# Reordered work at the seams of the 15-product passes and the down groups of a hybrid trunk kernel

## The reference, cut to what matters

```python
def swiglu(x, w_gate, w_up, w_down):
    return (jax.nn.silu(x @ w_gate) * (x @ w_up)) @ w_down
...
    h = x + 0.5 * swiglu(rmsnorm(x, ffn1_norm), ffn1_w_gate, ffn1_w_up, ffn1_w_down)
    p = rmsnorm(h, mix_norm) @ w_in
```

## Time and profile before

| what | us |
|---|---|
| runs | 1909.55, 1913.75, 1920.72 (median 1913.75) |
| profiled execution, device time | 1914.03 |
| its span | 1911.2 |
| first stage, until PE stops | 183.6 |
| passes, from PE's first matmul to the last | 197.28 to 518.8 |
| down groups | 518.8 to 840.3 |
| all behind them | 840.3 to 1911.2 |

### The profile page before, as it was taken

The page is one execution under the profiler, slowest core; times in us unless marked ns, Lnnn a source line. Parts: engine busy times, 40 slices in busy tenths (PEclk is TensorE's granted clock), DMA queues, the critical chain, the costliest instruction groups (busy, mean ns, idle before and its releaser), DMA issues.

```text
span 1911.2 us, 31212 instructions
## 1 busy us (share of the span) xinstructions
PE 1778.4 (93%) x11761; PEld 1755.1 (92%) x11761; DVE 1293.3 (68%) x2145; ACT 680.0 (36%) x1269; POOL 772.6 (40%) x767
## 2 busy tenths in 40 slices
PE   8998799999767777799999999999999999999998
PEld 8998799999657777799999999999999999999998
DVE  7264677776755555466257755997778877887775
ACT  7211444444322222235221153543333333333333
POOL 2697455555383233321079812223323333233320
PEclk9999899999878888899999999999999999999999
DMA  5432223222522022124811170111111111112112
GB/s 151 167 117 87 83 72 91 77 64 92 188 78 78 25 84 80 56 67 175 153 35 46 55 226 12 51 45 52 53 52 51 50 51 51 55 45 61 45 41 104
DMA packets 182358, 151.43 MB, mean 79 GB/s; under 512 B 11538, under 2 KB 175698, under 8 KB 181188
## 3 DMA queue, kind: packets, MB, share of 16 engines
q1 hardware_dynamic: 176724, 141.80, 24.3%
q0 software_dynamic: 864, 5.28, 0.8%
q10 hardware_dynamic: 4624, 2.36, 0.5%
HBM read 117.86 MB, written 31.57 MB: 78 GB/s over the span
## 4 chain that ended last, share of the span: by engine, by line
PE 74%; POOL 11%; DVE 5%; DMA 4%; issue 3%; ACT 2%; SPq 0%; DVEq 0%; POOLq 0%; ACTq 0%
PE bank_pair L1502 20%; PE bank_pair L1504 20%; PE bank_pair L1503 20%; PE bank_down L1502 4%; PE bank_down L1504 4%; PE bank_down L1503 4%; POOL PROD L3757 3%; DMA GW_raw<-in_ffn_w_down 3%; POOL UF_raw L3896 1%; POOL BS L3757 1%; POOL CA L3757 1%; ACT GS_hi L2329 1%; DVE GH_lo L3098 1%; POOL GS_raw L3903 1%; POOL TMP L3757 1%
## 5 line engine op out<-in xcount | busy, mean ns | idle before, releaser
L1502 PE MATMUL bank_pair<-XHM,U_hi 128*128 128x344 f32 x720 | 230.4, 320 | 0.2 <-DVE XLM L2870 0.2
L1504 PE MATMUL bank_pair<-XHM,U_lo 128*128 128x344 f32 x720 | 229.7, 319 | 0.0
L1503 PE MATMUL bank_pair<-XLM,U_hi 128*128 128x344 f32 x720 | 229.7, 319 | 0.0
L1502 PEld LDWEIGHTS bank_pair<-XHM,U_hi 128*128 128x128 f32 x720 | 135.2, 188 | 0.6 <-DVE XLM L2870 0.5
L1503 PEld LDWEIGHTS bank_pair<-XLM,U_hi 128*128 128x128 f32 x720 | 135.2, 188 | 0.0
L1504 PEld LDWEIGHTS bank_pair<-XHM,U_lo 128*128 128x128 f32 x720 | 135.2, 188 | 0.0
L1502 PE MATMUL bank_pair<-XF_hi,UF_hi 128*128 128x344 f32 x340 | 111.4, 328 | 21.7 <-DVE UF_lo L3033 13.7
L1502 PE MATMUL bank_pair<-GH_hi,GS_hi 128*128 128x344 f32 x160 | 59.5, 372 | 69.0 <-DVE HT L3120 69.0
L1502 PE MATMUL bank_pair<-XH,WH 128*128 128x344 f32 x384 | 123.6, 322 | 0.1
L3240 DVE SCALAR_TENSOR_TENSOR HT<-bank_pair,HT 128x344 f32<-128x344 f32 x210 | 103.5, 509 | 28.3 <-PE bank_pair L1504 28.0
L1503 PE MATMUL bank_pair<-XL,WH 128*128 128x344 f32 x384 | 122.5, 319 | 0.0
(11 more groups left out here) (487 smaller groups left out, 5855.3 us busy)
## 6 DMA issues: line engine op xcount, KB each, us to landing
GW_raw<-in_ffn_w_down SPq DMA_DIRECT2D x20, 512.0 KB, 3.5
GH_raw<-h_scratch SPq DMA_DIRECT2D x25, 344.0 KB, 6.0
RAW<-in_w_in SPq DMA_DIRECT2D x16, 512.0 KB, 4.3
UN<-in_ffn_w_gate SPq DMA_DIRECT2D x30, 256.0 KB, 3.6
UN<-in_ffn_w_up SPq DMA_DIRECT2D x30, 256.0 KB, 3.1
DQ_raw<-in_ffn_w_down SPq DMA_DIRECT2D x30, 256.0 KB, 2.8
h_scratch<-SA SPq DMA_DIRECT2D x40, 172.0 KB, 2.0
U_raw<-in_ffn_w_gate SPq DMA_DIRECT2D x22, 256.0 KB, 2.9
```

What stands on the lines that cost most here:

```text
L1502: pe.matmul(out, wh, xh, start=first, stop=False, skip_group_check=onto)
L1503: pe.matmul(out, wh, xl, start=False, stop=False, skip_group_check=onto)
L1504: return pe.matmul(out, wl, xh, start=False, stop=last, skip_group_check=onto)
```

## The change

It reorders the lists of all engines around three places and moves one piece of work.

- The turns of table C go from POOL to DVE (`c_turn`, eight of them, between the muls of f = 1 and 2). DVE's reciprocal moves ahead of the muls of f = 1. SP stores table C, and loads the first raw units inside its loop over f. POOL makes the table of powers behind table B instead of behind the fourth quarter.
- The last DVE and ACT items of the first stage make the parts of the first three steps; the five late x forms are spread over the first eight steps. In each step copies and adds come before the parts, and muls lag one step. R12 is before R11.
- In the last steps the group's first parts come one step later or more, SP's loads and stores of the last pass are in a list of their own, and in the groups ACT and DVE take the sums of quarter k+1 instead of k+2, ACT with quarter_high(k+2) behind group_high. BY_POOL is empty; the instructions that go by it are not made.

```diff
-PASS_ORDER = ("R1", "R2", "R9", "R4", "R6", "R3", "R7", "R0", "R5", "R8", "R13", "R14", "R11", "R12")
+PASS_ORDER = ("R1", "R2", "R9", "R4", "R6", "R3", "R7", "R0", "R5", "R8", "R13", "R14", "R12", "R11")
...
-FINALS = {"R6": ((1, 0),), "R3": ((0, 0),), "R5": ((1, 1),), "R8": ((0, 2),), "R11": ((2, 1),), "R12": ((1, 2), (2, 2)),
+FINALS = {"R6": ((1, 0),), "R3": ((0, 0),), "R5": ((1, 1),), "R8": ((0, 2),), "R11": ((2, 1), (2, 2)), "R12": ((1, 2),),
...
+BY_POOL = ()
+GROUP_LOW = tuple(u for u in GROUP_FORMS if u not in BY_POOL)
...
+C_TURNS = 4 + 6 * 8
...
+            for f in range(FO):
+                if f + 1 < FO:
+                    load_first(0, f + 1)
+                    load_first(1, f + 1)
...
+                if f == 3:
+                    sp.wait_ge(c_done, C_TURNS)
+                    sp.dma_start(CAD, CA[:, :, :, :].rearrange("p g r n -> p (g r) n")).then_inc(ca_out, 16)
+                if f == FO - 2:
+                    sp.wait_ge(ca_out, 16)
+                    sp.wait_ge(bs_out, 32)
+                    for at in range(5):
+                        load_raw(0, at)
...
+            run_past("R1")
+            load_ht(0, 0, 2)
+            run_past("R9")
+            load_group_h(0, B22)
...
+            run_past("R3")
+            load_group_h(0, B11)
+            load_group_h(0, B21)
+            store_h(LAST, 0, 0)
+            run_past("R7")
+            load_group_w(0)
+            run_past("R0")
+            load_group_h(0, None)
+            store_h(LAST, 0, 1)
+            store_h(LAST, 1, 1)
...
+            run_past("R12")
+            load_ht(2, 5, DC)
+            run_past("R11")
+            load_group_h(0, B13)
+            sp.wait_ge(un_ready, len(RUN))
+            load_group_h(0, B23)
+            store_h(LAST, 2, 1)
+            store_h(LAST, 2, 2)
+            run_past(TAIL)
+            load_group_w(1)
+            for u in (B11, None, B22, B21):
+                load_group_h(1, u)
+            store_h(LAST, 2, 0)
             for m, j in ((0, 0), (2, 1), (2, 0)):
                 wait_stored(sp, m, j, TRIPLES)
             load_group_w(2)
...
                 if name == "R0":
-                    act.wait_ge(ca_out, 16)
+                    act.wait_ge(bs_out, 32)
                 if name == "R9":
                     act.wait_ge(w_split[1], FO)
...
                     silu(f, (0,))
                     if f == 1:
                         discretise()
+                    if f == 6:
+                        for i in range(3):
+                            run_hi(i)
                     silu(f, (1, 2))
-                    if f == 6:
-                        x_form_hi("R0")
...
-            for i in range(3):
-                run_hi(i)
-            x_form_hi("R13")
-            x_form_hi("R10")
             run_hi(3)
             tail = len(RUN)
+            late = {0: "R13", 1: "R10", 3: "R8", 5: "R11", 6: "R12"}
             for i in range(tail):
...
                 if i + 4 < tail:
                     run_hi(i + 4)
-                run_copies(i)
...
-                    x_form_hi("R12")
...
+                if i in late:
+                    x_form_hi(late[i])
+                if i == tail - 5:
                     quarter_high(0)
-                if i == tail - 5:
+                if i == tail - 4:
                     group_high(0, B11)
+                if i == tail - 3:
+                    group_high(0, T1)
                     sums_high(0)
...
+                if i == tail - 2:
                     group_high(0, B21)
-                if i == tail - 3:
                     group_high(0, T2)
-                    group_high(0, B22)
...
+            quarter_high(1)
             for k in range(4 * GROUPS):
                 g, q = divmod(k, 4)
-                if k == 0:
-                    quarter_high(1)
-                    sums_high(1)
-                if k + 2 < 4 * GROUPS:
-                    quarter_high(k + 2)
-                    sums_high(k + 2)
+                if k + 1 < 4 * GROUPS:
+                    sums_high(k + 1)
                 if g + 1 < GROUPS and q > 0:
                     for u in GROUP_FORMS[3 * (q - 1):3 * q]:
                         group_high(g + 1, u)
+                if k + 2 < 4 * GROUPS:
+                    quarter_high(k + 2)
                 if k == 4 * GROUPS - 2:
...
+            def c_turn(n):
+
+                cr, ci = (AP8[:, 7, what, :].rearrange("p (g o) -> p g o", o=1).broadcast_to([P, GP, C16]) for what in range(2))
+                x, y = (CA[:, :, ri, (n - 1) * C16:n * C16] for ri in range(2))
+                before = 4 + 6 * (n - 1)
+                dve.wait_ge(c_done, before)
+                for out, part, turn in zip(CTMP, (x, y, y, x), (cr, ci, cr, ci)):
+                    dve.tensor_tensor(out[:, :, :], part, turn, ALU.mult).then_inc(c_done, 1)
+                dve.wait_ge(c_done, before + 2)
+                dve.tensor_tensor(CA[:, :, 0, n * C16:(n + 1) * C16], CTMP[0][:, :, :], CTMP[1][:, :, :], ALU.add
+                                  ).then_inc(c_done, 1)
+                dve.wait_ge(c_done, before + 4)
+                dve.tensor_tensor(CA[:, :, 1, n * C16:(n + 1) * C16], CTMP[2][:, :, :], CTMP[3][:, :, :], ALU.subtract
+                                  ).then_inc(c_done, 1)
+
...
                 dve.wait_ge(disc_p, 2)
                 dve.reciprocal(TMP[:, 12, :], TMP[:, 7, :]).then_inc(den_inv, 1)
+                c_turn(1)
+                c_turn(2)
+                mul(1, 0)
+                c_turn(3)
+                mul(1, 1)
+                c_turn(4)
+                mul(1, 2)
                 first_split(1, 2)
+                for n in range(5, 9):
+                    c_turn(n)
                 first_split(0, 3)
-                for tb in range(TB):
-                    mul(2, tb)
-                first_split(1, 3)
...
                 x_restore("B00", 0, 0)
+                mul(2, 0)
                 x_restore("B10", 1, 0)
                 x_step("R3", raw["R3"], b["B10"], b["B00"], "B10")
+                mul(2, 1)
                 x_restore("B02", 0, 2)
                 x_step("R7", raw["R7"], b["B02"], b["B00"], "B02")
-                first_split(0, 4)
...
                 first_split(1, 4)
                 x_form_lo("R3")
                 x_form_lo("R7")
                 x_restore("B01", 0, 1)
+                dve.wait_ge(bs_out, 32)
...
                 first_split(0, 5)
-                dve.wait_ge(bs_out, 32)
...
                 x_form_lo("R9")
                 x_form_lo("R0")
-                mul(6, 1)
-                run_lo(0)
-                run_lo(1)
-                mul(6, 2)
+                for i in range(2):
+                    run_lo(i)
+                for tb in range(TB):
+                    mul(6, tb)
+                run_lo(2)
...
             ffn_first()
-            x_form_lo("R13")
...
             tail = len(RUN)
...
+                run_adds(i)
                 if i + 3 < tail:
                     run_lo(i + 3)
-                run_adds(i)
-                if i == 0:
-                    x_form_lo("R8")
-                if i == 1:
...
+                if i in late:
+                    x_form_lo(late[i])
+                if i > 0:
...
+                    run_muls(i - 1)
                 if i == tail - 5:
                     group_mix(0, T1)
+                if i == tail - 4:
                     group_low(0, B11)
-                if i == tail - 4:
                     group_mix(0, T2)
+                if i == tail - 3:
                     group_mix(0, T4)
+                    group_low(0, T1)
+                if i == tail - 2:
+                    group_mix(0, T3)
                     sums_low(0)
-                if i == tail - 3:
-                    group_mix(0, T3)
-                    group_low(0, T1)
-                    group_low(0, B21)
-                if i == tail - 2:
-                    group_low(0, T2)
-                    group_low(0, B22)
-            group_low(0, B13)
-            group_low(0, B23)
-            group_low(0, T3)
-            group_low(0, T4)
+            run_muls(tail - 1)
+            for u in GROUP_LOW[2:]:
+                group_low(0, u)
             for n in range(GROUP_STEPS):
                 k, name = GROUP_RUN[n]
                 g, q = divmod(k, 4)
                 group_add(n)
-                if name == "M1" and k == 0:
-                    sums_low(1)
-                if name == "M3" and k + 2 < 4 * GROUPS:
-                    sums_low(k + 2)
+                if name == ("M3" if k else "P2") and k + 1 < 4 * GROUPS:
+                    sums_low(k + 1)
                 if g + 1 < GROUPS:
...
-            for j in range(1, 9):
-                rotate(ca(0, j), ca(1, j), ca(0, j - 1), ca(1, j - 1), ar, ai, -1)
-
-            pool.dma_start(CAD, CA[:, :, :, :].rearrange("p g r n -> p (g r) n")).then_inc(ca_out, 16)
+            pool.wait_ge(c_done, C_TURNS)
+
...
+            square_of((t(3), t(4)), t(5), t(6))
...
```

(41 more changed lines are left out.)

173 lines of the change are left out of this document (63 added, 110 removed).

## The result

The changed kernel takes **1822.3 us** (median of 4 runs, 1821.4 to 1824.7); the kernel before took 1913.0 in the same comparison (4 runs, 1909.6 to 1920.7). The ratio is 0.9523, with a 95% interval of 0.9492 to 0.9553: 91 us off, where 121 were forecast.

What follows compares the result with a forecast made beforehand. PE, busy 93% of the span, was taken as the bound, its losses mostly in groups and passes. Terms -96.5 + 15 - 13.7 - 10.7 - 6.9 - 9.9 = -122.7 from 1914.0 gave 1792 us, range 1768 to 1828.

Steps and rivals of the forecast that it cites:

- rival 2: Down groups: VectorE, not PE, sets the quarter at 12 us; 32 us more, 1824 us; chance 0.15.
- Groups, -96.5: Down groups: reordered ACT and DVE lists let PE set quarters of 10.3 us; 225 us with extras, against 321.5.
- C table, +15: First stage: turns moved to DVE cost 5.0 us each beside POOL, making the stage 15 us late; bounds 0 to +27.
- Rival 1: First stage: turns are cheap, 2.3 us each, and the stage is not late; 1777 us; chance 0.25.
- the two forecast stops: First stage: PE waits for FW_lo behind the turns, 3.2 us in tile 2, then until the stage is 13.6 us late.
- Behind it DVE has slack: First stage after the turns: DVE works 25.5 of 45.3 us, so the lateness is passed on and doesn't grow.
- Gap ahead of the passes, -13.7: Between first stage and passes: PE goes straight from the last up tile into R1, so the 13.7 us gap goes.
- Passes, -10.7, -6.9 and -9.9: Ten passes: PE's losses fall to 7 us at the start, 2 from 300 to 500, and 2.5 at the end.
- SP's queue is rewritten here: End of the passes: SP's reordered loads and stores hold back group 1's loads, wanted only 18 us later; no cost.
- Nine low parts by VectorE, nothing: Down groups: all nine low parts being DVE's is no edit, since BY_POOL is empty; no gain or loss.
- Rivals 2 and 3: Rival 3: both the longest turns in the first stage and somewhat late quarters in the groups; 1819 us; chance 0.07.
- Rival 4: Down groups: the loop through the weight load doesn't open, quarters of 16.5 us and more; 1925 us; chance 0.015.

Runs made afterwards that it cites:

- run 4: Changed kernel with the down groups' lists on ACT and DVE back to two quarters ahead, all else kept: 1908.7 us, against 1822.3 for the changed kernel.
- Run 5: Changed kernel with SyncE issuing the loads of B13 and B23 ahead of HT's load: 1815.7 us, against 1822.3 for the changed kernel.
- run 3: Changed kernel with POOL starting its B table only when all eight turns of the C table are done: 1823.1 us, against 1822.3.
- run 7: Changed kernel with turns 7 and 8 moved behind later low parts and FW_lo of tile 4 moved forward: 1806.0 us, against 1822.3.
- run 1: Changed kernel with SyncE issuing the sixth raw load of the next pass ahead of the store of block (1,2): 1808.0 us, against 1822.3.
- Runs 10 and 11: Changed kernel with load ahead, HT last, turns spread, later T2 form; low parts T3 and T4 on GpSimd (10) or all nine on VectorE (11): 1790.3 and 1790.5 us.

## Why the prediction was partly right

The direction and the mechanism that carries it were right, the size was 30 us too good. The measured time lies within the stated range, 1768 to 1828, only because of the bound that rival 2 set; the forecast by itself reached from 1780 to 1806. Point by point, by the sum:

- **Groups, -96.5.** It was -87.2, and undoing the order of ACT's and DVE's lists alone gives back 86 us (run 4). PE sets the quarter inside a group: from 550 to 600 us it makes 306 matmuls at clock 1.00 with one stop of 1.67 us, so a quarter of 66 takes 10.4 us, forecast 10.3. Of the miss of 9.3 us, 7.8 are at the start, a term that was named and mis-sized. The prediction had B13 and B23 behind HT, but took 8.5 us and 1.6 for the clock in all. Measured, from 513.17 to 550 us, PE lost 36.8 - 121 x 0.1565 = 17.9: the stops at 515.22, 517.57, 527.42 and 539.99 are 0.94 + 1.17 + 8.67 + 2.12 = 12.9, the other 5.0 are matmuls at the lower clock (0.77 granted in this stretch). Run 5 shows the share of the queue in it. Three of the four group changes cost 1.67, 1.98 and 1.50 us, close to the 1.5 forecast for each, the fourth nothing; there SyncE's list has no loads of h (`g + 2 < GROUPS`), which the prediction overlooked. It had no term for the table of powers either, and what its move gives is not known (run 4).
- **C table, +15.** It was +11.4. A turn costs 4.8 us, forecast 5.0, and 2.13 alone, forecast 2 to 2.3: the reading that two engines on two SBUF inputs take turns instruction by instruction holds for short ones too (run 3). The price was not quite made as forecast: DVE pays not its own time + 0.5 us but POOL's beat of 0.80 us, less than the two instructions alone add up to (0.36 + 0.74). The Trainium skill states (SBUF — State Buffer, SBUF: two separate sides) that VectorE with two SBUF inputs and a GpSimd instruction that reads SBUF lock each other out of their common ports for a whole instruction; the trace agrees in so far as neither gets two instructions through in one of the other's. Rival 1, cheap turns, is refuted. The first turn took 3.5 us, as POOL had only small work then, and two of the three muls between the turns cost nothing (turn and mul together take 4.8 us again), so FW_lo of tile 2 was there at 81.7 and the first of the two forecast stops (3.2) didn't come; the second was 9.16 for 10.4. "Behind it DVE has slack" was right too, and worth more than the prediction made of it: run 7 puts two turns into that slack and the whole +11.4 is gone.
- **Gap ahead of the passes, -13.7.** Right: the first R1 matmul (195.01) comes 0.16 us behind the last FW one.
- **Passes, -10.7, -6.9 and -9.9.** These failed. By the prediction's measure PE lost 105.0 - 586 x 0.1565 = 13.3 us up to 300, 200 - 1171 x 0.1565 = 16.7 from 300 to 500, and 13.2 - 50 x 0.1565 = 5.3 at the end; forecast were 7, 2 and 2.5. The step at fault is the one on SyncE: "SP's queue is rewritten here", which I read for what stands behind the wait for R10 and priced at nothing. I didn't read it in the loop over the passes. There the swap of R12 and R11 had put the store of (1, 2) ahead of a load, and the lag of the muls made that store later: four stops of 3.4 to 3.8 us, 14.9 us of the passes with the lower clock (run 1). That is the larger part of the 24 us by which the passes missed. In run 1 PE still loses 9.0, 6.1 and 5.6 us by the same measure, to 300 us, to 485 and to the end, 9 us above the forecast; its small stops ahead of R6 and that of R10 are a part of them, and the rest has no cause shown. R10's stop fell from 10.24 to 4.00, where 2.5 had been left for all of the end. Runs 10 and 11 show what it is: a form of the next stage, beside POOL, ahead of the addition in DVE's list.
- **Nine low parts by VectorE, nothing.** Right, since the kernel before has them too; and nine are within 0.3 us of seven (runs 10 and 11).
- **Rivals.** Rivals 2 and 3 give the measured time (1824, 1819) by mechanisms that aren't there, quarters of 12 us, turns of 6.5; the number alone would have confirmed them. The mean quarter is 234.3 / 20 = 11.7 us, near rival 2's, but inside a group it is 10.4. Rival 4 is refuted by the measured time and by run 4: the loop opened.

With the three local causes mended the kernel takes 1790.3 us, and that is near the 1792 of the sum. That is partly chance: the first stage then ends 15 us earlier than in the sum (183.1 for 198.6), the passes and groups take 10 and 4 us more (304.4 for 294, 228.9 for 225).

## What to carry to other kernels

When an order is changed, read every in-order list for pairs of a load and a store, the DMA queue's inside the loops above all: a store waits for the end of something, and a load behind it inherits that wait, in each round. Where work is moved to an engine that has slack on average, spread it between the instructions that others wait for, and price it at the rate beside the engine it collides with. A gain that one stage gives back at the next is no gain: moving work within a full list only moved the stop, while moving it into idle time, or a load ahead of a store, took it away.

## What the runs showed of the hardware

- A 128x256 tensor_tensor of VectorE on SBUF takes 0.36 to 0.42 us alone and 0.78 to 0.97 beside a chain of GpSimd instructions of its own size (0.7 to 0.8 us each): a factor of 2.3 for the whole turn (4.8 for 2.13). GpSimd pays much less: 0.80 us from one to the next for 0.74.
- One instruction can pay for most of a long one of the other engine: 128x688 on VectorE took 3.02 us for 0.86, begun 0.5 us behind one of GpSimd's of 2.80 us.
- Of two loads of 344 KB issued 0.5 us behind one of 1.58 MB, the one that was waited for landed after 7.97 us, and after 4.65 when issued ahead of it.
